# A hybrid decoder layer with a 32-expert MoE on one core: a pair's combine moved into the next pair, and another order of loads and transposes at the start

## What is computed

```python
proj = x @ w_in + b_in                      # 1024 -> 6144: u, v (GELU), p, q, gates
v = layer_norm(v, ln_v_g, ln_v_b)           # spatial gating, pooling, cross-attention follow
h = gates[..0] * br_a + gates[..1] * br_b + gates[..2] * br_m
x1 = layer_norm(ALPHA * x + h @ w_o, ln1_g, ln1_b)
# MoE: router picks 4 of 32 experts for each token
h = xb @ w1[e] + b1[e]                      # 1024 x 2048
g = min(h[:, :1024], 7); lin = clip(h[:, 1024:], -7, 7)
act = g * sigmoid(1.702 * g) * (lin + 1)
out = act @ w2[e] + b2[e]                   # 1024 x 1024
y = layer_norm(ALPHA * x1 + sum(gate * out), ln2_g, ln2_b)
```

## Time and profile before

| what | value |
|---|---|
| time, median of 3 runs | 1365.1 us (1358.51 to 1366.34) |
| profiled execution, its own time | 1363.53 us |
| its span (first to last instruction) | 1361.7 us |
| mean granted TensorE clock | 0.968 |
| PE, DVE, ACT, POOL busy | 93%, 31%, 20%, 16% |
| read from HBM | 461.51 MB |

### The profile page before, as it was taken

How to read it: one execution, slowest core, us unless ns; L and a number is a source line. 1 busy time by engine, 2 the same in 40 slices (tenths; PEclk the granted TensorE clock), 3 DMA queues, 4 the chain that set the end, 5 groups by cost and what they waited for, 6 DMA issues and landing times.

```text
span 1361.7 us, 15979 instructions
## 1 busy us (share of the span) xinstructions
PE 1265.5 (93%) x6436; PEld 733.5 (54%) x6436; DVE 420.1 (31%) x782; ACT 268.8 (20%) x375; POOL 223.9 (16%) x96
## 2 busy tenths in 40 slices
PE   6999999998979999999999999999999999999994
PEld 5989879998943434344343434434344343434431
DVE  3480373274631212212121221212122131221215
ACT  3433443333230111101011110111101011110111
POOL 5545257765420000000000000000000000000001
PEclk9979999998959999999899999999999999999997
DMA  9434584741469999999999999999999999999971
GB/s 314 154 121 154 170 277 150 226 155 62 164 276 414 418 431 426 427 430 425 410 418 429 427 427 430 429 427 429 428 428 429 427 429 429 427 430 429 411 325 40
DMA packets 77178, 464.78 MB, mean 341 GB/s; under 512 B 5554, under 2 KB 44006, under 8 KB 52465
## 3 DMA queue, kind: packets, MB, share of 16 engines
q1 hardware_dynamic: 72432, 456.67, 82.2%
q0 software_dynamic: 1456, 5.11, 1.3%
q10 hardware_dynamic: 3256, 2.53, 0.7%
HBM read 461.51 MB, written 2.90 MB: 341 GB/s over the span
## 4 chain that ended last, share of the span: by engine, by line
PE 83%; DVE 9%; ACT 4%; issue 2%; ACTq 1%; POOL 1%; DVEq 0%; POOLq 0%
PE ps L1563 33%; PE ps L1599 17%; PE ps L1257 15%; PE ps L1612 7%; PE ps L1268 2%; PE ps L1575 2%; DVE gs L1170 2%; DVE gm L1166 2%; DVE act_s L1173 2%; ACT sg L754 2%; ACT actT L759 1%; PE ps L1242 1%; PE ps L1349 1%; PE ps L1546 1%; PE ps L1358 1%
## 5 line engine op out<-in xcount | busy, mean ns | idle before, releaser
L1563 PE MATMUL ps<-big,xg 128*64 128x512 f32 x2048 | 456.2, 593 | 0.0
L1563 PEld LDWEIGHTS ps<-big,xg 128*64 128x64 f32 x2048 | 203.7, 137 | 220.1 <-issue 194.1
L505 POOL TENSOR_TENSOR ring_lo<-ring,w_hi 128x2048 fp32r<-128x2048 f32 x40 | 188.0, 4702 | 136.3 <-ACT w_hi L590 125.4
L1599 PE MATMUL ps<-big,actT 128*64 128x512 f32 x768 | 179.4, 618 | 14.9 <-ACT actT L759 14.9
L548 POOL TENSOR_TENSOR yacc<-yacc,ln 128x512 f32<-128x512 f32 x2 | 3.3, 1642 | 961.0 <-ACT yacc L612 961.0
L1166 DVE TENSOR_SCALAR gm<-ps 128x512 f32<-128x512 f32 x32 | 22.1, 692 | 412.5 <-PE ps L1563 412.5
L754 ACT ACTIVATE sg<-gm 128x512 f32<-128x512 f32 x32 | 20.2, 632 | 535.0 <-DVE gm L1166 535.0
L1599 PEld LDWEIGHTS ps<-big,actT 128*64 128x64 f32 x768 | 54.1, 141 | 117.5 <-issue 97.2
L1148 DVE COPY ypair<-ps 64x512 f32<-64x512 f32 x32 | 22.2, 694 | 253.7 <-PE ps L1599 253.7
L1612 PE MATMUL ps<-ypair,pickT 128*128 128x512 f32 (+1 forms) x192 | 91.6, 611 | 3.4 <-DVE ypair L1148 3.4
L590 ACT CAST w_hi<-ring 128x2048 fp32r<-128x2048 f32 x39 | 74.0, 1901 | 52.0 <-PE ps L1257 28.6
(11 more groups left out here) (271 smaller groups left out, 1174.8 us busy)
## 6 DMA issues: line engine op xcount, KB each, us to landing
big<-in_w SPq DMA_DIRECT2D x176, 2048.0 KB, 14.0
spare<-in_w SPq DMA_DIRECT2D x16, 2048.0 KB, 16.6
ring<-in_w_in SPq DMA_DIRECT2D x24, 1024.0 KB, 6.2
ring<-in_cache_mem_k SPq DMA_DIRECT2D x4, 1024.0 KB, 5.3
ring<-in_cache_mem_v SPq DMA_DIRECT2D x4, 1024.0 KB, 6.8
ring<-in_w_a_out SPq DMA_DIRECT2D x4, 1024.0 KB, 9.8
ring<-in_w_o SPq DMA_DIRECT2D x4, 1024.0 KB, 4.9
ring<-in_w_mk SPq DMA_DIRECT2D x2, 1024.0 KB, 5.3
```

The costliest lines, as they stand in the source:

```text
L505: pool.tensor_tensor(ring_lo[:, SLOTS[key] % HR, :], slot(*key), w_hi[:, SPLITS.index(key) % 2, :].bitcast(F32), ALU.subtract)\
L1563: ins = pe.matmul(ps[CAP * hh:CAP * hh + CAP, b, :], xg[:, k, par, :], big[:, w1_big, SLOT * kk + 512 * p:SLOT * kk + 512 * p + 512], star ...
L1599: ins = pe.matmul(ps[CAP * dh:CAP * dh + CAP, YB, :], actT[:, kk, j, :], w[:, kk, 512 * dh:512 * dh + 512], start=False, stop=(j == 1 and ...
```

## The change

**In the MoE.** The combine of pair n-1 is no longer behind that pair. Its parts 0 to 3 stand between the up products of pair n's first expert, one behind each of the k-steps 1 to 4, and parts 4 and 5 in that expert's activation gap, behind the gathered rows. DVE's adds stand at the matching places. The last pair's combine stands behind the loop, after the number of passes is loaded. The first pair is written out ahead of the loop (it has nothing to combine). The up bias matmuls move from the head of an expert into the activation gap of the one before. In the second expert's gap the turn of `pickg` moves ahead of the wait for act_s.

**At the start.** Seven small loads move from ACT's queue into SP's, behind the third and the sixth weight slot. ACT issues two DMAs, then runs a GELU on six columns of `ident`. Each tile of x has a semaphore of its own, and PE transposes tile by tile. DVE makes four of the xT_lo before w_hi of the first slot, and makes the first half of that slot's w_lo itself; POOL makes the other half.

```diff
-            for i, src in enumerate((a["ln_v_g"], a["ln_v_b"])):
-                act.dma_start(bvb[:, i, :], rows(src))\
-                    .then_inc(vparam_in, 16)
...
+            act.wait_ge(consts, 1)
+            act.activation(stats[:, 0, 0, :], ident[:, 0:6], ACT.Gelu_apprx_tanh)
...
+            for k in range(KD // 2):
+                x_lower(k)
+            dve.wait_ge(*loaded("v", 0))
+            dve.tensor_copy(w_hi[:, 0, :], slot("v", 0)).then_inc(w_high, 1)
+            for k in range(KD // 2, KD):
+                x_lower(k)
+            dve.wait_ge(w_high, 1)
+            dve.tensor_tensor(channels(ring_lo[:, 0, :], 0), channels(ring[:, 0, :], 0),
+                              channels(w_hi[:, 0, :], 0).bitcast(F32), ALU.subtract).then_inc(first_low, 1)
...
+            pe.wait_ge(consts, 1)
+            for tt in range(3):
+                pe.wait_ge(x_in[tt], 16)
+                for k in range(KD):
+                    ins = pe.transpose(opens("xT", k)[:, P * tt:P * tt + ROWS[tt]], x[0:ROWS[tt], tt, P * k:P * k + P],
+                                       ident[0:ROWS[tt], 0:ROWS[tt]])
+                    if tt == 2:
+                        ins.then_inc(*fills("xT", k))
...
+                        if par == 0 and not first and 1 <= k <= 4:
+                            combine_part(n - 1, k - 1)
 
                     gather_rows(g + 1, par)
+                    if par == 0 and not first:
+                        for t in (4, 5):
+                            combine_part(n - 1, t)
...
+                    up_bias(n + par, 1 - par)
...
-                pe.wait_ge(pickT_ready, n + 1)
-                pe.wait_ge(y_left_out, 2 * n + 2)
-                pe.wait_ge(y_right_out, 2 * n + 2)
-                for t in range(6):
...
-            dve.wait_ge(part_added, passes * (6 * PAIRS))
+            for t in range(6):
+                tt, dh = t // 2, t % 2
+                y = yacc[0:ROWS[tt], tt, 512 * dh:512 * dh + 512]
+                dve.wait_ge(last_done, t + 1)
+                dve.tensor_tensor(y, ps[0:ROWS[tt], O0 + t % 2, :], y, ALU.add).then_inc(last_added, 1)
+            dve.wait_ge(last_added, 6)
```

More of the change, by code:

```diff
@@ L364, in build @@
         PAIRS = NE // 2
+        UP_PARTS = [(GB, 0), (GB, 1), (LB, 0), (LB, 1)]
         HALF = D // 2
@@ L768, in _ @@
                 gathered(0, h)
-            with act.Fori(0, PAIRS) as i:
+            pair(0, 0)
+            with act.Fori(1, PAIRS) as i:
                 pair(0, i)
@@ L810, in inverse, with x_lower @@
                                          in1=rstd[r, tt:tt + 1], op0=ALU.mult, op1=ALU.mult).then_inc(rstd_ready, 1)
-            dve.wait_ge(*loaded("v", 0))
-            dve.tensor_copy(w_hi[:, 0, :], slot("v", 0)).then_inc(w_high, 1)
-            for k in range(KD):
+            def x_lower(k):
                 dve.wait_ge(*full("xT", k))
@@ L1161, in pair @@
                 ins.then_inc(pickg_ready, 1)
+                if not first:
+                    for t in range(4):
+                        add_part(n - 1, t)
                 for par in range(2):
@@ L1195, in _ @@
             dve.wait_ge(yacc_begun, 3)
-            with dve.Fori(0, PAIRS) as i:
+            pair(0, 0, first=True)
+            with dve.Fori(1, PAIRS) as i:
                 pair(0, i)
@@ L1532, in gather_turn, with up_bias, combine_part, pair @@
                 ins.then_inc(xg_done, 1)
-            def pair(q, i):
+            def up_bias(n, par):
+                pe.wait_ge(sel_ready, 2 * n + par + 1)
+                for p, (b, hh) in enumerate(UP_PARTS):
+                    pe.matmul(ps[CAP * hh:CAP * hh + CAP, b, :], sel[:, par, :], b1s[:, 512 * p:512 * p + 512],
+                              start=True, stop=False)
+            def combine_part(m, t):
+                tt, dh = t // 2, t % 2
+                if t == 0:
+                    pe.wait_ge(pickT_ready, m + 1)
+                    pe.wait_ge(y_left_out, 2 * m + 2)
+                    pe.wait_ge(y_right_out, 2 * m + 2)
+                if t >= 2:
+                    pe.wait_ge(part_added, 6 * m + t - 1)
+                pe.matmul(ps[0:ROWS[tt], O0 + t % 2, :], pickT[:, P * tt:P * tt + ROWS[tt]],
+                          ypair[:, 512 * dh:512 * dh + 512], start=True, stop=True).then_inc(part_done, 1)
+            def pair(q, i, first=False):
                 n = q * PAIRS + i
@@ L1620, in _ @@
             pe.wait_ge(ebias_ready, 1)
-            with pe.Fori(0, PAIRS) as i:
+            up_bias(0, 0)
+            pair(0, 0, first=True)
+            with pe.Fori(1, PAIRS) as i:
                 pair(0, i)
@@ L1633, in _ @@
                         pair(q, i)
+            pe.wait_ge(pickT_ready, passes * PAIRS)
+            pe.wait_ge(y_left_out, passes * NE)
+            pe.wait_ge(y_right_out, passes * NE)
+            for t in range(6):
+                tt, dh = t // 2, t % 2
+                if t >= 2:
+                    pe.wait_ge(last_added, t - 1)
+                pe.matmul(ps[0:ROWS[tt], O0 + t % 2, :], pickT[:, P * tt:P * tt + ROWS[tt]],
+                          ypair[:, 512 * dh:512 * dh + 512], start=True, stop=True).then_inc(last_done, 1)
 _INS = ['x_prompt', 'x_sample', 'state_pool', 'cache_mem_k', 'cache_mem_v', 'mem_prompt', 'w_in', 'b_in', 'ln_v_g',
```

94 lines of the change are left out of this document (48 added, 46 removed).

## The result

The changed kernel takes 1344.15 us (median of four, 1343.22 to 1345.13); the kernel before, run beside it, took 1361.8 (1357.44 to 1366.34). The ratio is 0.987, 95% interval 0.9829 to 0.9911. Forecast were 1346.5 and a range of 1339 to 1356. Faster by 1.3%, then, though by the interval a gain under 1% isn't quite excluded. The four runs of the kernel before are two near 1358 and two near 1366, so its median hangs on how many of each came; against the lower two the gain is 1.0%. One run that stands further down, of the start alone, took 1859.76 us at a mean granted clock of 0.65 and enters no number here. The profiled execution took 1345.13 us with a span of 1343.3, 18.4 less than the span before.

The account below looks back on a forecast made before the run. The prediction took the DMA engines' expert loads to bound the MoE loop, not PE. From 1363.5 us, -6.3 - 1.3 - 9.7 - 1.1 + 0.6 + 0.8 = -17.0 gave 1346.5 us, range 1339 to 1356.

Parts of the forecast that it names:

- DMA is the bound: MoE loop: expert loads set the pace at 58.7 us a pair; PE would need 56.0, so its cut gains nothing there.
- the four parts, 3.5: Loop, PE: four combine parts between up products cost at most 0.95 us each, 3.5 in all.
- within about three pairs: Loop: PE falls onto the DMA engines' pace within about three pairs, then waits for loads.
- one pause: Load stream in the loop: with more loads queued one pause goes, -1.3 us, bounds -6 and +3.
- rival 4: Loop: PE's waits for w1 blocks let the clock drop to 1.2 GHz, making the kernel slower, 1403 us; chance 0.06.
- The last expert, -9.7: Last expert: PE done 5.2 to 5.3 us behind the last landing instead of 15.0; bounds -7 and -10.
- lands at L - 9.8: Last expert: its fourth w1 block lands 9.8 us ahead of the last landing L, and PE's remaining work follows from there.
- The start, -6.3: Kernel start: first product begins at 12.8 us instead of 19.14; bounds 0 and 7.5 us of gain.
- Transposes keep their 7.36 us: Start, PE: the transposes of x take 7.36 us as before, from 4.2 to 11.6.
- DVE's half of w_lo, 1.2: Start, DVE: its 1024 columns of the first slot's w_lo take 1.2 us, done at 15.6.
- Rival 2: Start: v 0 or x isn't earlier, so 2.4 us or nothing of the 6.3 is gained, 1350.4 to 1352.8; chance 0.18.
- Behind the loop: After the last down product: DVE's idle time goes, -1.1 us; PE's load and branch ahead of the last combine add +0.6.

Follow-up runs that it names:

- the start alone: Kernel before with only the changed start (load order, tile-wise transposes, early GELU, split of the first slot) and the old MoE: 1358.19 us, ratio 0.9973.
- filled gap: Kernel before plus four idle matmuls per pair in the first expert's activation gap, nothing taken out: 1355.35 us, ratio 0.9938.
- transposes by channel: Changed kernel with PE's transposes of x again channel block by channel block behind all of x: 1347.83 us, ratio 0.9891.

## Why the prediction was right, and where it wasn't

- **DMA is the bound.** Right. The leads of PE show it, and two experiments that change PE's work or the bytes alone. But PE stands 1.7 us a pair behind (57.05 against 58.75), not 2.7: I had taken 56.0. The mis-sized term is the four parts, 3.5 against 4 x 1.20 = 4.8; the other terms of the sum were 0.25 too high together. "Less where the add is no longer waited for" was right (0.86 against 0.95), but I put a change of shape at nothing in the sum (0.3 was the upper bound), and it is 0.17 each. So PE came down to the loads' pace in the sixth pair, not "within about three pairs".
- **The stream, "one pause" at -1.3.** The step that failed; measured -4.1. I had let one pause go, because a waiting PE would queue more loads. What went is the cause of most of them: the clock fell in gaps that PE had little to do in, freed buffers came late, and a queue that was short then ran dry. Parts 4 and 5 fill that gap. The filled gap alone gives 8.1 us, of which 4.6 lie in the stream and 3.1 in the lead that PE keeps at the end. I had the row (one pair at 0.94 and 417 GB/s) and named it as a pause and for rival 4, but didn't ask what let the clock fall there and whether the change would stop it.
- **The last expert, -9.7.** Measured -6.4. The step that failed is that the fourth w1 block "lands at L - 9.8" and binds. It lands there, but it doesn't bind, because PE is still busy with expert 30. This error of 3.3 and the stream's 2.8 cancel, so that the MoE's -10.7 against -11.0 is luck.
- **The start, -6.3.** Measured -7.2, on other grounds in part, so part of the near hit is luck. "Transposes keep their 7.36 us": they take 4.17. "DVE's half of w_lo, 1.2": it takes 2.04 beside POOL's half, and is hidden behind the second step. What I had in my sum only as "nine DMA issues ahead" was the bound of the old start. Rival 2 is out: v 0 landed at 10.2, x's tiles at 4.5, 6.2 and 7.3.
- **Behind the loop**, -0.5: right, as PE's load and branch cost 0.5 of the 0.6 that I took.
- **Of the 18.4 us** the filled gap holds 8.1, the start 7.2, and the combine's move itself 3.1 (925.5 - 922.9 in the MoE, 0.5 behind it).

## What to carry to other kernels

Where two engines run within 3% of each other, ask first which one can't be made faster and how much lead the other has at the end; a cut on the second is worth that lead and no more. A gap in which TensorE idles a us or two can cost a second time through the clock (here 1.7 to 2.9 us behind four of 16 gaps, beside 1.8 of idle time): put the work that stands bare elsewhere into it, and where there is none, try idle matmuls. Keep DMA issues off an engine that has work at the start, and read the chain of the first 20 us by itself: the span's chain doesn't show it.

## What the runs showed of the hardware

- Behind a gap of 4.3 us in which PE was idle for 1.13 and 0.68 us, the granted clock fell to half in 3 or 4 of 16 pairs. With 1.6 us of idle matmuls in it the clock stayed at 1.00. Waits of up to 1.2 us on PE for a load, nine in the loop of the changed kernel, didn't lower it. The Trainium skill (TensorE: Matmul & The Clock Gate, "Loop structure matters more than you think") speaks of long waits between bursts; here much shorter ones did it.
- A DMA issue on ACT's queue took 0.4 to 0.6 us up to the fifth, and up to 5.8 with several ahead of it; on SP the third weight slot's issue took 3.7.
- A change between products of 64 and of 128 columns cost PE 0.17 us. Transposes in the order 128, 128 and 64 rows took 0.91 us for three; with the 16 of 128 rows first, all 24 took 4.17 instead of 7.35.
- DVE's subtraction of 1024 columns took 2.04 us with POOL's beside it and 1.22 without (in the kernel with transposes by channel).
